# Roots on ScalarE straight from the banks of sums, their table loaded before the last square, and five residual rows stored in place

## The reference

```
def _rms(x, g):
    x32 = x.astype(jnp.float32)
    y = x32 * lax.rsqrt(jnp.mean(x32 * x32, axis=-1, keepdims=True) + EPS)
    return (y * g.astype(jnp.float32)).astype(x.dtype)
...
h = _rms(x, norm1_g[i]) * (1.0 + sc1) + sh1
q = _rms(t[..., 0:W].reshape(Bt, Lt, NA_HEADS, HEAD_DIM), q_g)
x = x + g2 * _swiglu(h, ffn_w_gate[i], ffn_w_up[i], ffn_w_down[i])
h = jnp.concatenate([jnp.broadcast_to(meta.astype(x.dtype)[None], (B, N_META, D_MODEL)), x], axis=1)
```

## Time and profile before

| | us |
|---|---|
| median of 3 runs | 2271.29 (2266.49 to 2272.56) |
| the profiled execution | 2264.22 |
| its span | 2262.4 |
| TensorE busy | 2148.9 (95%) |
| VectorE busy | 1388.8 (61%) |
| ScalarE busy | 928.5 (41%) |
| GpSimd busy | 303.9 (13%) |

### The profile page before, as it was taken

How to read it: one execution, slowest core, us unless ns; L and a number is a source line. 1 busy time by engine, 2 the same in 40 slices (tenths; PEclk the granted TensorE clock), 3 DMA queues, 4 the chain that set the end, 5 groups by cost and what they waited for, 6 DMA issues and landing times.

```text
span 2262.4 us, 36561 instructions
## 1 busy us (share of the span) xinstructions
PE 2148.9 (95%) x13378; PEld 1830.2 (81%) x13378; DVE 1388.8 (61%) x2401; ACT 928.5 (41%) x1412; POOL 303.9 (13%) x325
## 2 busy tenths in 40 slices
PE   6999999999989998999999999997799999999998
PEld 3655788888876658999997788996688999999997
DVE  4546543442279564664767534998866666666666
ACT  3245422222243353444475204447633444444443
POOL 0022000000013030000000005787700000000000
PEclk9999999999989999999999999999999999999999
DMA  8266233223262364555543234550055555555553
GB/s 312 92 242 214 75 103 99 96 93 102 93 166 72 126 223 146 186 178 186 204 149 112 89 131 154 171 181 27 2 193 187 189 188 188 186 186 188 186 188 123
DMA packets 92851, 340.81 MB, mean 151 GB/s; under 512 B 10409, under 2 KB 10436, under 8 KB 92496
## 3 DMA queue, kind: packets, MB, share of 16 engines
q1 hardware_dynamic: 89280, 325.10, 42.5%
q0 software_dynamic: 3472, 14.35, 2.1%
HBM read 338.36 MB, written 1.05 MB: 150 GB/s over the span
## 4 chain that ended last, share of the span: by engine, by line
PE 55%; issue 29%; DVE 9%; ACT 3%; POOL 2%; DMA 1%; POOLq 0%; DVEq 0%; SPq 0%; ACTq 0%
PE banks L807 18%; PE banks L854 8%; PE banks L1070 6%; PE banks L972 4%; PE banks L556 4%; POOL tail_zone L2395 2%; DVE main_zone L1747 2%; DVE main_zone L1625 2%; PE banks L886 2%; DVE first_w_parts L1628 2%; PE banks L946 1%; PE banks L595 1%; PE banks L758 1%; PE banks L779 1%; PE banks L821 1%
## 5 line engine op out<-in xcount | busy, mean ns | idle before, releaser
L807 PE MATMUL banks<-act_parts,first_w_parts 128*128 128x512 f32 (+1 forms) x2592 | 478.8, 346 | 5.4 <-DVE act_parts L1628 4.6
L807 PEld LDWEIGHTS banks<-act_parts,first_w_parts 128*128 128x128 f32 x2592 | 411.7, 191 | 69.0 <-issue 9.1
L1145 PE MATMUL banks<-w_parts,a_parts 128*128 128x512 f32 x1536 | 367.5, 392 | 4.3 <-DVE a_parts L1628 3.2
L1628 DVE TENSOR_TENSOR first_w_parts<-weight_ring,first_w_parts 128x1024 fp32r<-128x1024 f32 x166 | 211.3, 1275 | 255.6 <-ACT first_w_parts L1300 255.6
L1145 PEld LDWEIGHTS banks<-w_parts,a_parts 128*128 128x128 f32 x1536 | 283.8, 189 | 60.1 <-issue 5.0
L1628 DVE TENSOR_TENSOR w_parts<-weight_ring,w_parts 128x1024 fp32r<-128x1024 f32 x219 | 267.4, 1221 | 90.0 <-ACT w_parts L1300 90.0
L1300 ACT ACTIVATE w_parts<-weight_ring 128x1024 fp32r<-128x1024 f32 x219 | 231.2, 1057 | 201.1 <-PE banks L1133 134.6
L1133 PEld LDWEIGHTS banks<-n_parts,w_parts 128*128 128x128 f32 x2184 | 273.9, 192 | 7.0
L1133 PE MATMUL banks<-n_parts,w_parts 128*128 128x256 f32 x2184 | 276.1, 283 | 0.0
L1300 ACT ACTIVATE first_w_parts<-weight_ring 128x1024 fp32r<-128x1024 f32 x166 | 174.7, 1056 | 223.8 <-PE banks L807 120.1
L854 PE MATMUL banks<-ffn_hidden_parts,first_w_parts 128*128 128x512 f32 (+1 forms) x1056 | 183.4, 336 | 0.0
(11 more groups left out here) (252 smaller groups left out, 2803.7 us busy)
## 6 DMA issues: line engine op xcount, KB each, us to landing
weight_ring<-in_stream SPq DMA_DIRECT2D x618, 512.0 KB, 3.3
main_zone<-in_rel_bias POOLq DMA_DIRECT2D x6, 512.0 KB, 12.4
main_zone<-in_decay POOLq DMA_DIRECT2D x1, 1536.0 KB, 9.5
main_zone<-in_xT POOLq DMA_DIRECT2D x1, 1024.0 KB, 11.4
main_zone<-in_ctxT POOLq DMA_DIRECT2D x1, 1024.0 KB, 15.9
tail_zone<-in_rel_bias POOLq DMA_DIRECT2D x2, 512.0 KB, 23.6
tail_zone<-in_keysT POOLq DMA_DIRECT2D x1, 1024.0 KB, 5.2
out<-main_zone SPq DMA_DIRECT2D x2, 512.0 KB, 2.6
```

The costliest lines, as they stand in the source:

```text
L807: mm = pe.matmul(o[:, 0:w], wb[:, hw, k, :], fin[:, hx, k, 0:w], start=(k == 0 and n == 0), stop=(k == DC - 1 and n == 2))
L1145: mm = pe.matmul(acc[n][:, :], ap_[:, e % 3, ha, (n // 2) * P:(n // 2 + 1) * P], wp[(B + b) % PARTS][:, hw, (n % 2) * 512:(n % 2 + 1) * 51 ...
L1628: return dve.tensor_tensor(o, a, b, op)
```

## The change

- VectorE's scale-and-add between sum and root is gone, in the six norms and in the 21 chunks of queries and keys. ScalarE's root reads the bank and takes the scale as a constant and EPS as its bias, from a new column `eps` of the small tables. In the last norm of all, the scale moves into the root too, the addition of two columns stays.
- With it go the semaphores `var_ready` and `qk_sums_read`. TensorE's waits for `qk_sums_read` are now for `qk_std`, the root. A root of layer 1 from chunk 2 on also waits for `qk_normed` of the chunk two before, whose place it takes; attention of layer 1 waits for `qk_normed` of all chunks.
- The table load by a root of one column stands in `square` ahead of the wait for the last row, for k = 1 to 5.
- For k = 4, rows 3 to 7 of the residual are written to `HR` by the last addition of layer 1's FFN, and squared from there; the copy takes rows 0 to 2 and stands behind the reciprocal.

```
 def square(k, c):
+    if c == DC - 1:
+        act.activation(stat[:, 3, 0:1], ones[:, 0:1], ACT.Sqrt)
     evacuated(act, BEFORE[k], c + 1)
     if k == 4:
-        act.activation(norms[4]["sq"][:, c, META:LT], X[:, c, 0:L], ACT.Square).then_inc(squares_ready, 1)
+        act.activation(norms[4]["sq"][:, c, META:LT], HR[:, c, META:LT] if c >= 3 else X[:, c, 0:L],
+                       ACT.Square).then_inc(squares_ready, 1)
...
-    act.wait_ge(var_ready, k + 1)
+    act.wait_ge(sumsq_ready, k + 1)
     w = d["n"] // 4
-    act.activation(rstd[:, 0:w], rstd[:, 0:w], ACT.Sqrt).then_inc(std_ready, 1)
+    act.activation(rstd[:, 0:w], bank[6][:, 0:w], ACT.Sqrt, bias=small("eps"), scale=1.0 / D).then_inc(std_ready, 1)
...
 def qk_root(l, j):
     c, w, g, sq_at, r_at = CHUNKS[l][j]
-    act.wait_ge(qk_sums_read, sum(QKN[:l]) + j + 1)
-    r = view(r_at, w)
-    act.activation(r, r, ACT.Sqrt).then_inc(qk_std, 1)
+    n = sum(QKN[:l]) + j
+    act.wait_ge(qk_sums, n + 1)
+    if l == 1 and j >= 2:
+        act.wait_ge(qk_normed, n - 1)
+    act.activation(view(r_at, w), bank[4 + n % 2][:, 0:w], ACT.Sqrt, bias=small("eps"),
+                   scale=1.0 / HD).then_inc(qk_std, 1)
...
 def norm(k):                                   # VectorE
-    dve.wait_ge(sumsq_ready, k + 1)
     w = n // 4
-    ts(rstd[:, 0:w], bank[6][:, 0:w], 1.0 / D, EPS, ALU.mult, ALU.add).then_inc(var_ready, 1)
+    dve.wait_ge(std_ready, k + 1)
+    dve.reciprocal(rstd[:, 0:w], rstd[:, 0:w]).then_inc(rstd_ready, 1)
     if k == 4:
         dve.wait_ge(meta_in, 16)
         dve.tensor_copy(HR[:, :, 0:META], meta)
-        dve.tensor_copy(HR[:, :, META:LT], X[:, :, 0:L]).then_inc(x_ready, 1)
+        dve.tensor_copy(HR[:, 0:3, META:LT], X[:, 0:3, 0:L]).then_inc(x_ready, 1)
         dve.wait_ge(x_ready, 1)
-    dve.wait_ge(std_ready, k + 1)
-    dve.reciprocal(rstd[:, 0:w], rstd[:, 0:w]).then_inc(rstd_ready, 1)
-    if k == 4:
         low_mix(1)
...
 # qk_norm, VectorE
-    dve.wait_ge(qk_sums, base + j + 1)
-    ts(r, bank[4 + (base + j) % 2][:, 0:w], 1.0 / HD, EPS, ALU.mult, ALU.add).then_inc(qk_sums_read, 1)
     dve.wait_ge(qk_std, base + j + 1)
     link(dve.reciprocal(r, r))
...
 # last addition of the FFN, VectorE
-    last = stt(X[:, m, a:e], b[:, a:e], MOD[:, l, 40 + m, s:s + 1], X[:, m, a:e], ALU.mult, ALU.add)
+    x = HR[:, m, META:LT] if l == 1 and m >= 3 else X[:, m, a:e]
+    last = stt(x, b[:, a:e], MOD[:, l, 40 + m, s:s + 1], X[:, m, a:e], ALU.mult, ALU.add)
```

More of the change, by code:

```diff
@@ L165 @@
 SMALLS = [("ident", 128), ("ones", 128), ("block", 128), ("perm", 128), ("iota", 128), ("iota16", 16),
-          ("pick", 12), ("strip", 4)]
+          ("pick", 12), ("strip", 4), ("eps", 1)]
 SM = {}
@@ L299, in build @@
         sumsq_ready = sem("sumsq_ready")
-        var_ready = sem("var_ready")
         std_ready = sem("std_ready")
@@ L317, in build @@
         qk_sums = sem("qk_sums")
-        qk_sums_read = sem("qk_sums_read")
         qk_std = sem("qk_std")
@@ L664, in fourier @@
                 evacuated(pe, "ev_in", 10)
-                pe.wait_ge(qk_sums_read, QKN[0])
+                pe.wait_ge(qk_std, QKN[0])
                 for u in range(8):
@@ L703, in qk_sum @@
                 if n >= 2:
-                    pe.wait_ge(qk_sums_read, n - 1)
+                    pe.wait_ge(qk_std, n - 1)
                 pe.matmul(bank[4 + n % 2][:, 0:w], block64, view(sq_at, w), start=True, stop=True).then_inc(qk_sums, 1)
@@ L747, in attention @@
                 u0 = l * PAIRS
-                pe.wait_ge(qk_ready, l + 1)
+                if l == 0:
+                    pe.wait_ge(qk_ready, 1)
+                else:
+                    pe.wait_ge(qk_normed, QKN[0] + QKN[1])
                 pe.wait_ge(vt_copied, [1, 9][l])
@@ L1335, in ffn @@
                             high_mix(0)
-                            act.activation(stat[:, 3, 0:1], ones[:, 0:1], ACT.Sqrt)
                         square(4, m)
@@ L1599, in final_root @@
                 act.wait_ge(yvar_ready, tt + 1)
-                act.activation(stat[:, 1, tt:tt + 1], stat[:, 1, tt:tt + 1], ACT.Sqrt).then_inc(ystd_ready, 1)
+                act.activation(stat[:, 1, tt:tt + 1], stat[:, 1, tt:tt + 1], ACT.Sqrt, bias=small("eps"),
+                               scale=1.0 / D).then_inc(ystd_ready, 1)
             for n in range(4):
@@ L1642, in first_norm @@
                 w = T // 4
-                dve.wait_ge(sumsq_ready, 1)
-                ts(rstd[:, 0:w], bank[6][:, 0:w], 1.0 / D, EPS, ALU.mult, ALU.add).then_inc(var_ready, 1)
                 dve.wait_ge(std_ready, 1)
@@ L1749, in qk_norm @@
                     last = stt(p, p, par("qkg", g), r, ALU.mult, ALU.mult)
-                    if l == 0:
-                        last.then_inc(qk_normed, 1)
+                    last.then_inc(qk_normed, 1)
                 for b in range(split, count):
@@ L1754, in qk_norm @@
                 if l == 1:
-                    last.then_inc(qk_ready, 1)
                     return
@@ L2283, in final_mean @@
                 v = stat[:, 1, tt:tt + 1]
-                link(tt_(v, stat[:, 0, 2 * tt:2 * tt + 1], stat[:, 0, 2 * tt + 1:2 * tt + 2], ALU.add))
-                ts(v, v, 1.0 / D, EPS, ALU.mult, ALU.add).then_inc(yvar_ready, 1)
+                tt_(v, stat[:, 0, 2 * tt:2 * tt + 1], stat[:, 0, 2 * tt + 1:2 * tt + 2], ALU.add).then_inc(yvar_ready, 1)
             def final_rows(tt):
@@ L2422, in tables @@
     smalls[:, SM["ones"]:SM["ones"] + P] = 1
+    smalls[:, SM["eps"]] = EPS
     smalls[:, SM["block"]:SM["block"] + P] = np.kron(np.eye(2), np.ones((64, 64)))
```

## The result

The changed kernel took 2256.70 us (median of 5 runs, 2253.25 to 2258.20); the kernel before, in the runs beside it, 2266.49 (5 runs, 2266.10 to 2272.56). The ratio is 0.9938 with a 95% interval of 0.9921 to 0.9956: faster by 10 to 18 us. The profiled execution took 2253.25 us, its span is 2251.4 us against 2262.4, 11.0 us less.

A forecast was written before the change was run, and what follows sets the result against it. TensorE is busy 95% of the span, but VectorE was taken to set layer 1's query and key norm. Gains 8.4 + 2.6 + 0.6 + 0.4 = 12.0 us off 2271.29 gave 2259.3 us, range 2254 to 2267.

The forecast's parts named there:

- layer 1's stage: Layer 1's query and key norm: 8.1 us at the sixth wide tile plus a 0.29 us wait, 8.4 us gained.
- 677.64 + 2.1 + 20.6 = 700.3: Sixth wide tile's start: GpSimd begins 2.1 us later for one more DMA block; the low part ends 20.6 after that.
- the same 12.0 off the median gives 2259.3: Whole kernel: the 12.0 us gain taken off the median of the runs, 2271.29 us.
- The clock's 2.0 us: Layer 1's tile at 700.09: 2.0 us lost to a lower granted clock before, counted as gone.
- So VectorE sets this stage: Layer 1's norm: VectorE's cycle, 6.58 us wide and 4.23 narrow, exceeds TensorE's 6.36 and 3.30.
- Norms 1, 2, 3 and 5: Root directly behind the sums, table load moved ahead of the last square: 2.6 us gained, after 0.3 lost in norm 5.
- No drain: Moved table loads: a 1380 ns drain, if it came, would cost some 3 us, leaving a gain of about 9.
- Norm 4 and the end: Norm 4, less scale-and-add and copying but a wait for the root: 0.6 us gained; last norm's root: 0.4.
- rival 5: Layer 1's stage: GpSimd is no hindrance, total gain 14.6 us, 2256.7 us; chance 0.12.
- rivals 1 and 4: Layer 1's stage: 1, GpSimd's additions and clock, gain 4.3 us, chance 0.13; 4, clock stays at 1.2 GHz, slower, chance 0.03.
- rival 2: Layer 1's stage: ScalarE replaces VectorE as the bound, total gain 3.6 us, 2267.7 us; chance 0.05.
- rival 3: Norms 1, 2, 3 and 5: moved table loads are late, 3.0 us lost, gain 9.0, 2262.3 us; chance 0.05.

The follow-up runs named there:

- the first set of experiments: Follow-up runs of the unedited changed kernel and other versions beside the kernel before (2269.37 us); the changed kernel took 2254.51 us, ratio 0.9941.
- the repeat: The changed kernel, unedited, run and profiled once more: 2254.51 us, ratio 0.9941 to the kernel before.
- late additions: Changed kernel with GpSimd's four additions of mask and bias held back until behind layer 1's projection: 2248.84 us, ratio 0.9913.
- late additions again: The changed kernel with GpSimd's four mask additions held back, run a second time: 2254.48 us, ratio 0.9929.
- norms only: The changed kernel with the query and key norms put back as before, so norms, rows and end remain: 2263.36 us, ratio 0.9976.
- the query-and-key part alone: The kernel before with only layer 1's and layer 0's query and key norms changed: 2260.49 us, ratio 0.9960.
- the kernel before with late additions: The kernel before with GpSimd's four mask additions held back by one more wait: 2261.94 us, ratio 0.9967.

## Why the prediction came out as it did

Two steps failed. The first is the base that the gain was taken off: 2271.29 us, where all five runs give 2266.49. The second is the size of one term, layer 1's stage: 8.4 us forecast, 9.34 measured. It went by 677.64 + 2.1 + 20.6 = 700.3 for the sixth wide tile, and the trace has 677.37 + 22.0 = 699.4. A last part, the 1.3 us between the trace's 12.7 and the ratio's 14.0, stays open.

The gain forecast was 12.0 us. The trace gives 9.34 + 2.42 + 0.46 + 0.44 = 12.7 of the change's own; the 1.78 us that the profile lost in layer 0 is the run's. The ratio's interval (10 to 18 us) holds both.

**The base.** The step "the same 12.0 off the median gives 2259.3" took 2271.29 us, a median of three runs of which one was 2266.49. The median of all five is 2266.49, and by the ratio the changed kernel is then at 2252.4: below my range of 2254 to 2267. As a ratio I forecast 2259.3 / 2271.29 = 0.9947, which lies within the interval. The range allowed 3 us for the scatter of a median; the kernel before had medians from 2266.49 to 2270.76 in four sets of runs and single runs from 2264.98 to 2277.10. In the first set of experiments the changed kernel had 2254.51 beside 2269.37.

**Layer 1's stage: right in the place, the size 0.9 too low, and one sentence wrong.** First wide tile: forecast 666.5, measured 666.68. That fits so well by luck: my walk started from 653.28 unchanged and left out the 2.1 us that norms 1 and 2 give ahead of it, and this execution had lost 1.78 in layer 0. The tile of 708.39: forecast 700.3, measured 699.43. Without GpSimd I had 698.3 for it, 0.6 too late for a walk from 653.28, since the first two wide tiles follow each other in 5.93 and 6.14 us and not in 6.36. The term that was mis-sized is GpSimd's: "677.64 + 2.1 + 20.6". The additions did not start 2.1 us later for the one more block (677.37; 676.11 in the repeat). I had assumed that they would catch the low part for the sixth wide tile. It ran behind them, in 1.21 us. It ended 22.0 us after they began, and not 20.6, because VectorE met them 4 us later (at 682.88, after waiting for a root) and a 512-wide reciprocal stands among the steps now. 677.37 + 22.0 = 699.4. TensorE's long wait stood in front of the fifth tile instead (1.25 us); the sixth started as its low part ended. The clock's 2.0 us went as forecast.

Of the 0.9 us, 0.55 are this tile's (0.31 of its gain came in from the norms and layer 0), 0.15 the next one's and 0.25 the values' projection's (0.54 where I had 0.3). The sentence "So VectorE sets this stage" was right for the narrow tiles (1.85 us) and wrong for the wide ones: with late additions TensorE goes at 6.35 us in both kernels. The sum did not rest on it, since I walked along TensorE's tiles and GpSimd's additions; but someone who had priced the wide cycle, 8 x 0.22 us, would have found 1.8 us and missed the 7.0. And TensorE's waits were ended not by the low part that the sentence names but by the scale-and-add behind it, 0.3 to 0.6 us later.

**Norms 1, 2, 3 and 5: 2.6 forecast, 2.4 measured, partly by luck.** Norm 1 gave 0.64, norm 2 1.45, norm 5 0.4. Norm 3's spread came 0.79 us earlier and its eight matmuls took 0.87 longer. TensorE there, in the changed kernel, in the second profile of the kernel before, and with late additions again:

```profile
870.11 1.97 PE L642 MATMUL banks<-small_zone 128*128 128x64 f32 x8 [1.01 <-DVE small_zone L1694]
```
```profile
883.43 1.97 PE L644 MATMUL banks<-small_zone 128*128 128x64 f32 x8 [1.84 <-DVE small_zone L1696]
```
```profile
873.85 1.10 PE L642 MATMUL banks<-small_zone 128*128 128x64 f32 x8 [1.02 <-DVE small_zone L1694]
```

The kernel before has 1.10 us in one profile and 1.97 in the other, and late additions again has 1.10 with the changed norms, so either can have either. The changed kernel has 1.97 in both of its profiles, and that this is not the change's doing is likely but not shown. Like against like, norm 3 gives 0.8 and the four together 3.3. I undervalued the early load (3.1 us alone by the run without it). Norm 5's last square was 0.3 us late, as forecast: VectorE was done at 1356.9 and the square began at 1357.23.

**No drain.** In the rows of norm 5 above the load starts 0.02 us behind the high parts and the next instruction 0.01 behind the load. The Trainium skill (ScalarE: Activation LUTs, What ACT_TABLE_LOAD costs) counts 1283 ns for the load, which agrees, and 1380 ns of drain beside it, which nothing here shows.

**Norm 4 and the end.** 0.6 forecast and 0.46 measured, 0.4 and 0.44. The copy of three rows took 0.68 us where my eighths made it 0.46.

**Rivals.** By the number alone rival 5 fits as well as the forecast: it had 14.6 us, and 14.0 with the 2.6 for the norms that the other sums use (its 3.2 is an error), and the ratio gives 14.0. The trace decides against it. The low clock of rivals 1 and 4 did not come in the stage; ScalarE (rival 2) made VectorE wait for roots (2.7 us), but no tile of TensorE waited for one and the wide tiles kept 6.35 us; the loads (rival 3) were in time. Rival 5, GpSimd no hindrance, was wrong by the 1.5 us that the additions still cost.

**Open.** The medians of "norms only" (5.4 us) and of late additions (up to 5.7 in one set) are above what their traces place (3.5 and 1.5). Granted clock that falls in other places from run to run can do it, as 90 to 120 us shows, but these runs don't show that it does.

## What to carry to other kernels

Before pricing a stage by the busiest engine's cycle, look at the tiles that waited and at what ran on GpSimd then: here a wide cycle 0.2 us too long cost nothing, a narrow one 0.9 too long cost 1.9 us, and four additions on an idle engine cost 8.5. What VectorE is ahead of TensorE when the additions begin is the slack that absorbs them, so a step less in each block pays here though the wide tiles never waited for its length, and moving the additions pays alike (one wait, 7.2 us in the kernel before by the medians). And take the base of a forecast from all runs there are: the base alone moved mine by 4.8 us.

## What the runs showed of the hardware

- Beside GpSimd's additions of two SBUF tiles, VectorE's multiply took 4.80 us instead of 0.48 and the low part 5.60 instead of 1.22. A tensor_scalar with one input in SBUF was caught too, 2.93 us instead of 0.29; the reciprocal was not (1.74 and 3.34). The Trainium skill (SBUF — State Buffer, Who interferes with whom) counts tensor_scalar among the operations that can enter a two-port mode, and the trace agrees.
- TensorE's clock falls in different places from execution to execution. In the profile of the kernel before with late additions the granted clock was 0.50 (its lower level, 1.2 GHz) for 10 us at the end of layer 1's attention, where the query-and-key part alone had 1.00. Windows of the latter, then of the former:

```profile
835.00:845.00 10.00, 9.95 (x54) 9.00 (x55) 1.54 (x5) 0.83 (x2) 0.00 (x0) 1.00 0.32 105
```
```profile
835.00:845.00 10.00, 8.92 (x45) 7.07 (x42) 0.58 (x2) 2.17 (x4) 0.00 (x0) 0.50 0.15 48
```

  Its gain of 7.96 us at the start of that attention was 2.53 at 850 us. This is not shown to be the edit's doing: the changed kernel with late additions lost nothing there in its first profile (1.00 in the same window) and 2.5 us in its second (0.84).
